# Narrow projections with the activations stationary, an earlier order of first loads, and a reordered ending, in a two-block transformer kernel on one core

## The chip, the cores and the metric

The kernel runs on one core of one Trainium2 chip. The metric is the device time of one execution in microseconds, from its first to its last instruction with what little lies around them. It was timed three times before the change: median 2977.05 us, from 2974.29 to 2977.88.

## The reference

Two blocks run one after the other on 256 tokens of width 2048. The change touches two small projections inside the large input projections, the first loads of the program and its last normalization. Cut to that:

```python
def first_block(x, p, ...):
    a_in = _rmsnorm(h, attn_norm_g[i])
    proj = a_in @ w_in[i]                     # z | xbc | dt_raw (32 columns) | q | k | v
    z, xbc, dt_raw, q, k, v = jnp.split(proj, [o1, o2, o3, o4, o5], axis=-1)
    dt = jax.nn.softplus(dt_raw.astype(jnp.float32) + dt_bias[i].astype(jnp.float32))
    ...                                       # SSM, attention, gated FFN, PLE

def second_block(x, g_mix, w_in, ...):
    h = rms_norm(x, g_mix[l])
    proj = h @ w_in[l]
    q, k, v, z, f, scal, gates = jnp.split(proj, SPLIT_POINTS, axis=-1)   # scal: 4 * 8 = 32 columns
    ...                                       # gated delta rule, Fourier branch, w_o
    h = rms_norm(x, g_mlp[l])
    x = x + jnp.square(jax.nn.relu(h @ w_mlp_up[l])) @ w_mlp_down[l]
    return rms_norm(x, g_final)
```

## The kernel before

**Tiling.** Tokens lie in TT = 2 tiles of P = 128 partitions, the width in KT = 16 k-tiles, outputs in chunks of NC = 512 columns, DC = 4 chunks to a width of 2048. Every float32 product is done as three fp32r products: the weights are split into w_hi (the cast, on ACT) and w_lo (the rest, on DVE), the activations into a_hi and a_lo, and hi x hi, lo x hi and hi x lo are summed in PSUM.

**The weight stream.** All large weights come in one stream of slabs, each 128 partitions x 1024 floats (512 KB), four slabs to a quad. SP issues a slab's transfer into w_raw when DVE has split the one before it in that place (lo_ready). ACT and DVE both have a `split`, for casts and for rests. PE's `slab` (L2154 to L2166) does the eight matmuls on w_hi (L2159), then the four on w_lo (L2164), with a 128x128 tile of the activations stationary and 512 weight columns moving, and counts slab_done. `chunk` runs eight slabs for one 512-column output, into a pair of PSUM banks (one for each token tile) that pair_free says are empty.

**Narrow projections.** The 32 columns of dt (first block) and the 32 of scal (second block) don't come with the stream. `narrow` on PE projects them between two chunks: the 32 weight columns are stationary, all 256 tokens move, 16 k-tiles x 3 products = 48 matmuls into a 32x256 result. ACT copies that to SBUF (narrow_T, L873; narrow2_T, L1121, semaphore narrow_copied), and PE transposes it to token rows with two transposes (L2241), after which narrow_t lets DVE and ACT read it. PE waits for ACT in the middle of that. In front of the first copy ACT evacuates a chunk and computes the sine and cosine of the rotary angles (L870, L871).

**Opening.** SP issues piece 0 of x (512 columns, 512 KB), slab 0, slab 1, piece 1, slabs 2 and 3, pieces 2 and 3, then eight small tensors. ACT's queue issues the identity, then the rows of the five column gains (gain_rows). POOL first issues load_gain(G_SSM), 1 MB, and then its memsets. PE waits for the identity and gain_rows, transposes the gains and then x (L2187), ACT scales the transposed tiles into a_hi (L784), DVE makes a_lo, ACT casts slab 0, and the first chunk starts.

**Ending.** The last quad is the second half of the last down projection. PE does chunks 0 and 1 of it slab by slab for both token tiles, then tile 0's chunks 2 and 3 and tile 1's chunks 2 and 3 (L2832 to L2834). For each (t, n) DVE adds the sum to h (`add_last_to_h`, L2111), ACT squares it with a row sum (`end_squares`, L1326), DVE multiplies by the final gain (`out_gain`, L2116); when the four squares of a tile are in, DVE makes the mean (L2120, L2121), POOL the root (L750), and ACT or DVE scales (L1330, L2144, L2146). All are in a fixed order on their engines, written out by hand. SP stores tile 0 and two chunks of tile 1, ACT the other two chunks as one transfer (L1349).

Of the kernel before, what the change touches and what calls it, by code (L numbers as in the profile page):

```python
# [25 lines left out]
ALU = mybir.AluOpType  # L26
AX = mybir.AxisListType


P = 128  # L30
SEQ, D = 256, 2048
TT = SEQ // P
KT = D // P
NC = 512
# [158 lines left out]
def program(nc, wstream, small, const, out):  # L193

    ctx = ExitStack()
    with ctx:
# [5 lines left out]
        def sem(name):  # L202
            sems[name] = ctx.enter_context(nc.semaphore(name))
            return sems[name]
# [147 lines left out]
        gain_rows = work[:, 0:P]  # L352
        narrow_T = sp[0:HEADS, 1:5].rearrange("p m n -> p (m n)")
        narrow2_T = s_cv[0:4 * DNH, 0]

# [90 lines left out]
        dve_step, pool_step = sem("dve_step"), sem("pool_step")  # L446
        narrow_mm, narrow_t, narrow_copied = sem("narrow_mm"), sem("narrow_t"), sem("narrow_copied")
        sp_abs, sp_exp, sp_sum, sp_ln = sem("sp_abs"), sem("sp_exp"), sem("sp_sum"), sem("sp_ln")
# [41 lines left out]
        def _(sp_):  # L490
# [5 lines left out]
            def first_slab(s):  # L496
                sp_.dma_start(w_raw[:, s, :], wstream[0, s]).then_inc(raw_loaded[s], 16)
            piece(0)
            first_slab(0)
            first_slab(1)  # L500
# [28 lines left out]


            sp_.wait_ge(out_scaled, DC)
            sp_.dma_start(out[0], xn_m[:, 0]).then_inc(stored, 16)
            for c in range(DC // 2, DC):
                cols = slice(c * NC, (c + 1) * NC)
                sp_.wait_ge(normed, NORMED[G_POST] + 2 * DC + c - DC // 2)
                sp_.dma_start(out[1, :, cols], xn_m[:, 1, cols]).then_inc(stored, 16)
            sp_.wait_ge(stored, (1 + 2 * DC + 2 + DC // 2) * 16)

        @block.gpsimd
        def _(pool):  # L540
            step = Chain(pool, pool_step)

            def load_gain(n):

                if n:
                    pool.wait_ge(normed, NORMED[n - 1])
                pool.dma_start(gain[:], small["gains"][N_COLUMN + n:N_COLUMN + n + 1, :].to_broadcast([P, D])).then_inc(gain_loaded, 16)
# [6 lines left out]
            def norm_root(n):  # L554

                pool.wait_ge(rstd_ready, 2 * n + 1)
                nc.gpsimd.tensor_tensor(rstd[:, n], rstd[:, n], neg_half[:, 0:TT], ALU.pow).then_inc(rstd_ready, 1)  # L557


            load_gain(G_SSM)  # L560
            for p in range(4):
# [5 lines left out]
            for s, n in [(pair_free[p], 2) for p in range(4)] + [(back_evac, 2), (back2_evac, 2), (dn_free, 2), (stored, 16)]:  # L567
                pool.wait_ge(s, n)
            norm_root(N_ATTN)


# [180 lines left out]
        def _(act):  # L752
# [89 lines left out]


            act.dma_start(ident[:], const["ident"]).then_inc(first_loaded, 16)
            act.dma_start(gain_rows, small["gains"].rearrange("n (k p) -> (n k) p", p=P)).then_inc(first_loaded, 16)
            act.wait_ge(gain_t, 1)
# [24 lines left out]
            nc.scalar.activation(cos[:], ang[:, 5], ACT.Sin).then_inc(rope_ready, 1)  # L871
            act.wait_ge(narrow_mm, 1)
            nc.scalar.copy(narrow_T[:], bank[7][0:HEADS, 0:SEQ]).then_inc(narrow_copied, 1)  # L873
            softplus_parts(1, sp)
# [232 lines left out]
            with act.Fori(0, 3) as i:  # L1107
                for k in range(2):
# [10 lines left out]
                    nc.scalar.copy(qkv2[:, 0, bass.ds(c * NC, NC)], bank[6][:]).then_inc(back2_evac, 1)  # L1119
            act.wait_ge(narrow_mm, 2)  # L1120
            nc.scalar.copy(narrow2_T[:], bank[5][0:4 * DNH, 0:SEQ]).then_inc(narrow_copied, 1)  # L1121

            q = Q_F + 2
# [198 lines left out]
            def end_squares(t, n):  # L1322

                act.wait_ge(pair_free[n % 2], 2 * (U_MLP + 2 * j + 2 - n % 2) + 2 * (n // 2) + t + 1)
                cols = slice(n * NC, (n + 1) * NC)
                nc.scalar.activation(xn_m[:, t, cols], h[:, t, cols], ACT.Square, accum_out=stat[:, t, n:n + 1]).then_inc(stat_ready, 1)  # L1326
# [11 lines left out]
            end_squares(0, 3)  # L1338
            act.wait_ge(normed, NORMED[G_POST] + 6)
            act.wait_ge(rstd_ready, 2 * (N_OUT + 1))  # L1340
            for c in range(DC):
                out_chunk(0, c)
            end_squares(1, 2)
            end_squares(1, 3)
            act.wait_ge(rstd_ready, 2 * (N_OUT + 2))
            for c in range(DC // 2):
                out_chunk(1, c)
            act.wait_ge(out_scaled, DC + DC // 2)
            act.dma_start(out[1, :, 0:D // 2], xn_m[:, 1, 0:D // 2]).then_inc(stored, 16)  # L1349

        @block.vector
        def _(dve):
# [764 lines left out]

            def end_mean_square(t):
                dve.wait_ge(stat_ready, TT * DC * N_OUT + 6 + 2 * t)
                step(V.tensor_reduce(mean[:, t:t + 1], stat[:, t], AX.X, ALU.add))  # L2120
                V.tensor_scalar(rstd[:, N_OUT, t:t + 1], mean[:, t:t + 1], 1.0 / D, EPS, ALU.mult, ALU.add).then_inc(rstd_ready, 1)  # L2121
            dve.wait_ge(gain_loaded, 16 * (G_OUT + 1))
            for n in range(2):
                split(N_QUADS - 1, 2 * n, 2 * n + 2)
                dve.wait_ge(slab_done, QUAD * (N_QUADS - 2) + 2 * (n + 1))
                for t in range(TT):
                    add_last_to_h(t, n)
                for t in range(TT):
                    out_gain(t, n)

            for t in range(TT):
                for n in range(2, DC):
                    dve.wait_ge(slab_done, QUAD * (N_QUADS - 1 + t) + 2 * (n - 1))
                    add_last_to_h(t, n)
                    if n == 2:
                        out_gain(t, n)
                end_mean_square(t)
                if t == 0:
                    out_gain(t, DC - 1)
            dve.wait_ge(rstd_ready, 2 * (N_OUT + 2))  # L2140
            for c in range(DC // 2, DC):
                cols = slice(c * NC, (c + 1) * NC)
                if c < DC - 1:
                    last = V.tensor_scalar(xn_m[:, 1, cols], h[:, 1, cols], rstd[:, N_OUT, 1:2], None, ALU.mult)  # L2144
                else:
                    last = V.scalar_tensor_tensor(xn_m[:, 1, cols], h[:, 1, cols], rstd[:, N_OUT, 1:2], gain[:, cols], ALU.mult, ALU.mult)  # L2146
                last.then_inc(normed, 1)
        @block.tensor
        def _(pe):
# [79 lines left out]

            def narrow(psum, hi, lo, width, done, token_major, transposed):  # L2230


                o = psum[0:width, 0:SEQ]
                for k in range(KT):
                    T.matmul(o, hi[:, k], a_hi[:, k], start=k == 0, stop=False)
                    T.matmul(o, lo[:, k], a_hi[:, k], start=False, stop=False)
                    last = T.matmul(o, hi[:, k], a_lo[:, k], start=False, stop=k == KT - 1)
                last.then_inc(done, 1)
                pe.wait_ge(narrow_copied, transposed)
                for t in range(TT):  # L2240
                    last = T.transpose(psum[:, SEQ + t * width:SEQ + (t + 1) * width], token_major[:, t * P:(t + 1) * P],  # L2241
                                       ident[0:width, 0:width])
                return last
# [28 lines left out]
            pe.wait_ge(narrow_lo_ready, 1)  # L2272
            narrow(bank[7], w32_hi, w32_lo, HEADS, narrow_mm, narrow_T, 1).then_inc(narrow_t, 1)
            with pe.Fori(0, 2) as i:
# [252 lines left out]
            pe.wait_ge(narrow_lo_ready, 2)  # L2527
            narrow(bank[5], s_hi, s_lo, 4 * DNH, narrow_mm, narrow2_T, 2).then_inc(narrow_t, 1)
            chunk(Q_F + 2, 1, U_F, a_hi, a_lo)
# [293 lines left out]
            for t in range(TT):  # L2823
                ts = slice(t * P, (t + 1) * P)
                for n in range(2, DC):
                    pe.wait_ge(pair_free[n % 2], 2 * (use + 3 - n % 2))
                    for i in range(2 * n - QUAD, 2 * n - QUAD + 2):
                        pe.wait_ge(lo_ready, QUAD * (N_QUADS - 1) + i + 1)
                        for k in range(SLAB_KT):
                            tile = 2 * (i % 2) + k  # L2830
                            wh, wl = (x[:, i, k * NC:(k + 1) * NC] for x in (w_hi, w_lo))
                            T.matmul(pair[n % 2][t][:], last_hi[:, tile, ts], wh, start=tile == 0, stop=False)  # L2832
                            T.matmul(pair[n % 2][t][:], last_lo[:, tile, ts], wh, start=False, stop=False)
                            last = T.matmul(pair[n % 2][t][:], last_hi[:, tile, ts], wl, start=False, stop=tile == 3)  # L2834
                        last.then_inc(slab_done, 1)
# [82 lines left out]
```

## Time and profile before

| what | us |
|---|---|
| median of three timed runs | 2977.05 (2974.29 to 2977.88) |
| the profiled execution's own time | 2975.56 |
| its span, first to last instruction | 2973.7 |
| PE busy in the span | 2937.8 |
| DVE busy | 2006.2 |
| ACT busy | 1419.0 |
| POOL busy | 318.5 |

PE is the matmul side of TensorE, PEld its weight loads, which can overlap. Busy time of a pipelined PE overlaps with itself, so that the start of one matmul to the start of the next says more than their durations: a row with x8 covers eight instructions from the start of the first to the end of the last. "Idle before" in brackets names what ended the idle time.

### The profile page before, as it was taken

What the parts mean: (1) busy time and instruction counts of PE and PEld (TensorE: products, weight loads), DVE (VectorE), ACT (ScalarE), POOL (GpSimd) and SP (SyncE); (2) the same over time, 40 slices, a digit from 0 to 9 for tenths busy, and PEclk for the clock granted to TensorE, in tenths of its full rate; (3) what the DMA queues carried; (4) which work ended last, traced back from release to release, by engine and by line L of the source; (5) the groups of instructions that cost most, each with busy time, mean ns of one, the idle gap of its engine ahead of it and who ended that gap; (6) DMA issues with size and microseconds to landing.
All of it is one profiled execution on the core that took longest, in us unless ns stands there. A gap on an engine that the chain in (4) does not pass through costs nothing.

```text
span 2973.7 us, 44205 instructions
## 1 busy us (share of the span) xinstructions
PE 2937.8 (99%) x15407; PEld 2412.2 (81%) x15407; DVE 2006.2 (67%) x2615; ACT 1419.0 (48%) x1838; POOL 318.5 (11%) x274
## 2 busy tenths in 40 slices
PE   8999999999999999999999999999999999999998
PEld 7888777788888888887888877777888888888887
DVE  6765767656677777667678677777655666666666
ACT  6444556644444444445555453344545444444444
POOL 0002970000000000000000064442000000000000
PEclk9999999999999999999999999999999999999999
DMA  6555443456555555554565533333765555555554
GB/s 217 179 188 173 135 168 125 157 194 213 184 188 186 179 194 186 194 190 142 185 226 176 182 114 122 122 123 119 242 218 192 189 191 187 188 190 190 185 191 147
DMA packets 145147, 525.80 MB, mean 177 GB/s; under 512 B 16416, under 2 KB 17184, under 8 KB 144160
## 3 DMA queue, kind: packets, MB, share of 16 engines
q1 hardware_dynamic: 139760, 503.72, 51.2%
q0 software_dynamic: 1536, 11.78, 1.1%
q10 hardware_dynamic: 3760, 9.05, 0.9%
q8 instruction: 62, 1.02, 0.1%
q14 instruction: 29, 0.24, 0.0%
HBM read 516.09 MB, written 8.39 MB: 176 GB/s over the span
## 4 chain that ended last, share of the span: by engine, by line
PE 93%; DVE 2%; POOL 2%; ACT 1%; issue 1%; DMA 0%; DVEq 0%; ACTq 0%; SPq 0%; POOLq 0%
PE bank L2159 56%; PE bank L2164 28%; PE bank L2256 1%; PE bank L2578 1%; PE bank L2187 1%; DVE w_lo L1360 1%; ACT w_hi L759 1%; PE bank L2607 0%; PE bank L2395 0%; POOL xs L602 0%; PE bank L2489 0%; POOL work L627 0%; PE bank L2264 0%; DMA w_raw<-weights 0%; PE bank L2804 0%
## 5 line engine op out<-in xcount | busy, mean ns | idle before, releaser
L1360 DVE TENSOR_TENSOR w_lo<-w_raw,w_hi 128x1024 fp32r<-128x1024 f32 x952 | 1192.2, 1262 | 784.1 <-ACT w_hi L759 783.2
L759 ACT CAST w_hi<-w_raw 128x1024 fp32r<-128x1024 f32 x952 | 1000.2, 1052 | 1400.5 <-PE bank L2164 1376.6
L2159 PE MATMUL bank<-w_hi,a_hi 128*128 128x512 f32 x2784 | 1109.6, 399 | 4.6 <-ACT w_hi L759 2.8
L2159 PE MATMUL bank<-w_hi,a_lo 128*128 128x512 f32 x2784 | 1087.0, 390 | 0.0
L2164 PE MATMUL bank<-w_lo,a_hi 128*128 128x512 f32 x2784 | 750.1, 390 | 0.0
L2159 PEld LDWEIGHTS bank<-w_hi,a_hi 128*128 128x128 f32 x2784 | 523.9, 188 | 121.2 <-issue 10.6
L2164 PEld LDWEIGHTS bank<-w_lo,a_hi 128*128 128x128 f32 x2784 | 523.1, 188 | 110.2
L2159 PEld LDWEIGHTS bank<-w_hi,a_lo 128*128 128x128 f32 x2784 | 524.5, 188 | 104.7 <-issue 1.9
L2159 PE MATMUL bank<-w_hi,m_hi 128*128 128x512 f32 x480 | 186.8, 389 | 0.0
L2159 PE MATMUL bank<-w_hi,m_lo 128*128 128x512 f32 x480 | 186.7, 389 | 0.0
L1432 DVE TENSOR_TENSOR h<-h,bank 128x512 f32<-128x512 f32 x232 | 148.5, 681 | 19.9 <-PE bank L2164 19.9
L2159 PE MATMUL bank<-w_hi,f_hi 128*128 128x512 f32 x352 | 138.8, 394 | 0.0
L2159 PE MATMUL bank<-w_hi,f_lo 128*128 128x512 f32 x352 | 137.1, 389 | 0.0
L557 POOL TENSOR_TENSOR rstd<-rstd,neg_half 128x2 f32<-128x2 f32 x6 | 4.3, 716 | 1214.8 <-DVE rstd L1389 1214.8
L2164 PE MATMUL bank<-w_lo,m_hi 128*128 128x512 f32 x480 | 128.4, 389 | 0.0
L2159 PEld LDWEIGHTS bank<-w_hi,m_hi 128*128 128x128 f32 x480 | 90.1, 188 | 18.7
L2164 PEld LDWEIGHTS bank<-w_lo,m_hi 128*128 128x128 f32 x480 | 90.1, 188 | 18.7
L2159 PEld LDWEIGHTS bank<-w_hi,m_lo 128*128 128x128 f32 x480 | 90.1, 188 | 18.6
L2164 PE MATMUL bank<-w_lo,f_hi 128*128 128x512 f32 x352 | 94.2, 390 | 0.0
L713 POOL TENSOR_TENSOR delta<-delta,level_sb 128x512 f32<-128x512 f32 x40 | 64.8, 1637 | 127.0 <-DVE delta L1947 122.6
L2164 PEld LDWEIGHTS bank<-w_lo,f_hi 128*128 128x128 f32 x352 | 66.1, 188 | 13.9
L2159 PEld LDWEIGHTS bank<-w_hi,f_lo 128*128 128x128 f32 x352 | 66.1, 188 | 13.5 <-issue 0.2
(410 smaller groups left out, 2520.1 us busy)
## 6 DMA issues: line engine op xcount, KB each, us to landing
w_raw<-weights SPq DMA_DIRECT2D x952, 512.0 KB, 4.0
gate<-gate_st ACTq DMA_DIRECT2D x8, 512.0 KB, 3.9
h<-gate ACTq DMA_DIRECT2D x8, 512.0 KB, 5.0
gain<-gains POOLq DMA_DIRECT2D x3, 1024.0 KB, 7.5
h<-x_tok SPq DMA_DIRECT2D x4, 512.0 KB, 10.8
w_proj_sb<-w_proj POOLq DMA_DIRECT2D x1, 2048.0 KB, 9.7
h_rest<-h POOLq DMA_DIRECT2D x1, 2048.0 KB, 8.6
h<-h_rest POOLq DMA_DIRECT2D x1, 2048.0 KB, 9.9
```

The source lines that it names most:

```text
L557: nc.gpsimd.tensor_tensor(rstd[:, n], rstd[:, n], neg_half[:, 0:TT], ALU.pow).then_inc(rstd_ready, 1)
L713: nc.gpsimd.tensor_tensor(hd.mk, hd.m, level[:, k].unsqueeze(1).to_broadcast(shape), ALU.mult).then_inc(dn_mk, 1)
L759: nc.scalar.copy(w_hi[:, s, :], w_raw[:, s, :]).then_inc(hi_ready, 1)
L1360: V.tensor_tensor(w_lo[:, s, :], w_raw[:, s, :], w_hi[:, s, :].bitcast(F32), ALU.subtract).then_inc(lo_ready, 1)
L1432: V.tensor_tensor(h[:, t, col], h[:, t, col], pair[p][t][:], ALU.add).then_inc(pair_free[p], 1)
L2159: T.matmul(psum[t][:], left[:, t * P:(t + 1) * P], wh, start=start and j == 0 and n == 0, stop=False)
L2164: last = T.matmul(psum[t][:], products[j][0][:, t * P:(t + 1) * P], wl, start=False, stop=stop and j == SLAB_KT - 1)
L2187: last = T.transpose(bank[4 + i % 4][:, k * SEQ + t * P:k * SEQ + (t + 1) * P], src[:, t, (2 * i + k) * P:(2 * i + k + 1) * P], ident[:])
L2256: last = T.transpose(bank[first + ct // 2][:, (ct % 2) * SEQ + t * P:(ct % 2) * SEQ + (t + 1) * P], src[:, t, col0 + ct * P:col0 + (ct + 1 ...
L2578: last = T.matmul(out[r, r], left[:, r], right[:, r], start=True, stop=True)
```

## The change

Five things are changed.

- `narrow` makes the activations stationary: for each k-tile and token tile three matmuls with a 128x128 tile of a_hi or a_lo loaded and the 32 weight columns moving, 96 in all, straight into token rows. The 32x256 result, ACT's two copies, the two pairs of transposes and the semaphores for them go.
- On ACT's queue gain_rows goes ahead of the identity, and slab 0 comes third; SP's queue no longer carries slab 0. POOL issues the load of the SSM gain after the first norm's root instead of first.
- On DVE the last adds, gains and splits are reordered: the adds of chunk 1 come ahead of the last two splits, several gains come later, tile 1's mean of the first three chunks is made ahead of its last add, and the last square is folded in by one instruction. DVE takes over tile 0's last output piece, with its gain.
- On ACT the square of (1, 2) comes ahead of tile 0's scalings, of which three remain. The stores of tile 1 become four of 256 KB, three on SP and one on ACT.
- PE's last chunks wait for one token tile's add instead of two, and start a pair of k-tiles' w_hi products before w_lo is ready.

```diff
@@ narrow
-                o = psum[0:width, 0:SEQ]
                 for k in range(KT):
-                    T.matmul(o, hi[:, k], a_hi[:, k], start=k == 0, stop=False)
-                    T.matmul(o, lo[:, k], a_hi[:, k], start=False, stop=False)
-                    last = T.matmul(o, hi[:, k], a_lo[:, k], start=False, stop=k == KT - 1)
-                last.then_inc(done, 1)
-                pe.wait_ge(narrow_copied, transposed)
-                for t in range(TT):
-                    last = T.transpose(psum[:, SEQ + t * width:SEQ + (t + 1) * width], token_major[:, t * P:(t + 1) * P],
-                                       ident[0:width, 0:width])
+                    for t in range(TT):
+                        o, ts = psum[:, SEQ + t * width:SEQ + (t + 1) * width], slice(t * P, (t + 1) * P)
+                        T.matmul(o, a_hi[:, k, ts], hi[:, k], start=k == 0 and t == 0, stop=False)
+                        T.matmul(o, a_lo[:, k, ts], hi[:, k], start=False, stop=False)
+                        last = T.matmul(o, a_hi[:, k, ts], lo[:, k], start=False, stop=k == KT - 1 and t == TT - 1)
@@ ACT, the copies
-            act.wait_ge(narrow_mm, 1)
-            nc.scalar.copy(narrow_T[:], bank[7][0:HEADS, 0:SEQ]).then_inc(narrow_copied, 1)
...
-            act.wait_ge(narrow_mm, 2)
-            nc.scalar.copy(narrow2_T[:], bank[5][0:4 * DNH, 0:SEQ]).then_inc(narrow_copied, 1)
@@ SP, POOL and ACT, opening
             piece(0)
-            first_slab(0)
             first_slab(1)
...
-            load_gain(G_SSM)
...
             norm_root(N_ATTN)
+            load_gain(G_SSM)
...
+            act.dma_start(gain_rows, small["gains"].rearrange("n (k p) -> (n k) p", p=P)).then_inc(first_loaded, 16)
             act.dma_start(ident[:], const["ident"]).then_inc(first_loaded, 16)
-            act.dma_start(gain_rows, small["gains"].rearrange("n (k p) -> (n k) p", p=P)).then_inc(first_loaded, 16)
+            act.dma_start(w_raw[:, 0, :], wstream[0, 0]).then_inc(raw_loaded[0], 16)
@@ SP, ending
+            sp_.wait_ge(out_scaled, DC - 1)
+            sp_.wait_ge(normed, NORMED[G_POST] + 6)
+            sp_.dma_start(out[0], xn_m[:, 0]).then_inc(stored, 16)
...
+            sp_.wait_ge(normed, NORMED[G_POST] + 8)
+            store(2)
             sp_.wait_ge(out_scaled, DC)
+            store(0)
+            sp_.wait_ge(normed, NORMED[G_POST] + 9)
+            store(3)
@@ ACT, ending
             end_squares(0, 3)
-            act.wait_ge(normed, NORMED[G_POST] + 6)
+            end_squares(1, 2)
+            act.wait_ge(normed, NORMED[G_POST] + 5)
             act.wait_ge(rstd_ready, 2 * (N_OUT + 1))
-            for c in range(DC):
+            for c in range(DC - 1):
                 out_chunk(0, c)
-            end_squares(1, 2)
             end_squares(1, 3)
             act.wait_ge(rstd_ready, 2 * (N_OUT + 2))
-            for c in range(DC // 2):
+            for c in range(2):
                 out_chunk(1, c)
-            act.wait_ge(out_scaled, DC + DC // 2)
-            act.dma_start(out[1, :, 0:D // 2], xn_m[:, 1, 0:D // 2]).then_inc(stored, 16)
+            act.wait_ge(out_scaled, DC + 1)
+            act.dma_start(out[1, :, NC:2 * NC], xn_m[:, 1, NC:2 * NC]).then_inc(stored, 16)
@@ DVE, ending (the new order)
+            split(N_QUADS - 1, 0, 2)
             for n in range(2):
                 dve.wait_ge(slab_done, QUAD * (N_QUADS - 2) + 2 * (n + 1))
                 for t in range(TT):
                     add_last_to_h(t, n)
+            split(N_QUADS - 1, 2, 4)
+            dve.wait_ge(gain_loaded, 16 * (G_OUT + 1))
             for t in range(TT):
+                out_gain(t, 0)
+            last_chunk_done(0, 2)
+            for t in range(TT):
+                out_gain(t, 1)
+            last_chunk_done(0, 3)
+            out_gain(0, 2)
+            dve.wait_ge(stat_ready, TT * DC * N_OUT + 6)
+            step(V.tensor_reduce(mean[:, 0:1], stat[:, 0], AX.X, ALU.add))
+            V.tensor_scalar(rstd[:, N_OUT, 0:1], mean[:, 0:1], 1.0 / D, EPS, ALU.mult, ALU.add).then_inc(rstd_ready, 1)
+            last_chunk_done(1, 2)
+            dve.wait_ge(rstd_ready, 2 * (N_OUT + 1))
+            out_piece(0, DC - 1, True)
+            out_gain(1, 2)
+            step(V.tensor_reduce(mean[:, 1:2], stat[:, 1, 0:DC - 1], AX.X, ALU.add))
+            step(V.tensor_scalar(mean[:, 1:2], mean[:, 1:2], 1.0 / D, EPS, ALU.mult, ALU.add))
+            last_chunk_done(1, 3)
+            dve.wait_ge(stat_ready, TT * DC * N_OUT + 8)
+            V.scalar_tensor_tensor(rstd[:, N_OUT, 1:2], stat[:, 1, DC - 1:DC], 1.0 / D, mean[:, 1:2], ALU.mult, ALU.add).then_inc(rstd_ready, 1)
             dve.wait_ge(rstd_ready, 2 * (N_OUT + 2))
+            out_piece(1, 2, False)
+            out_piece(1, 3, True)
@@ PE, last chunks
-                    pe.wait_ge(pair_free[n % 2], 2 * (use + 3 - n % 2))
+                    pe.wait_ge(pair_free[n % 2], 2 * (use + 3 - n % 2) - 1 + t)
```

## Rows read from the trace of the kernel before

**Rows 1.** The page: busy time and share by engine, and the chain that ended last
```profile
PE 2937.8 (99%) x15407; PEld 2412.2 (81%) x15407; DVE 2006.2 (67%) x2615; ACT 1419.0 (48%) x1838; POOL 318.5 (11%) x274
...
PE 93%; DVE 2%; POOL 2%; ACT 1%; issue 1%; DMA 0%; DVEq 0%; ACTq 0%; SPq 0%; POOLq 0%
```

**Rows 2.** Timeline around the first narrow projection: start us, us, engine line op
```profile
38.02 0.28 PE L2235 MATMUL bank<-a_hi,w_hi 128*32 128x256 f32 x1
...
46.59 0.80 PE L2159 MATMUL bank<-w_hi,a_hi 128*128 128x512 f32 x1
...
49.72 0.39 PE L2159 MATMUL bank<-w_hi,a_lo 128*128 128x512 f32 x1
```

**Rows 3.** Stretches: start:end, length, busy by engine, granted clock, DMA share, GB/s
```profile
43.79:46.25 2.46, 0.00 (x1) 0.01 (x1) 2.46 (x3) 2.41 (x6) 0.00 (x0) 1.00 0.64 201
46.59:49.60 3.01, 3.01 (x8) 2.43 (x8) 2.55 (x9) 2.20 (x3) 0.00 (x0) 0.50 0.91 302
...
1709.84:1712.43 2.59, 2.59 (x25) 2.59 (x24) 2.59 (x1) 2.32 (x2) 2.10 (x1) 1.00 0.02 6
```

**Rows 4.** Timeline around the second narrow projection
```profile
1657.94 1.07 PE L2164 MATMUL bank<-w_lo,a_hi 128*128 128x512 f32 x4
...
1659.64 0.36 PE L2235 MATMUL bank<-a_hi,s_hi 128*32 128x256 f32 x1
...
1665.94 0.20 PEld L2241 LDWEIGHTS bank<-ident_sb,s_cv 32*128 32x128 f32 x2 [0.73 <-ACT s_cv L1121]
...
1666.18 0.50 PE L2159 MATMUL bank<-w_hi,a_hi 128*128 128x512 f32 x1
```

**Rows 5.** Small products and weight loads: timelines, and groups (busy us, mean ns)
```profile
1710.20 0.37 PE L2537 MATMUL bank<-g,cum_sb 128*128 128x8 f32 x2
...
1711.98 0.60 PE L2541 MATMUL bank<-g,chunk_ones_sb 128*128 128x16 f32 x4
...
L2235 PEld LDWEIGHTS bank<-a_hi,w_hi 128*32 128x32 f32 x16 | 1.7, 108 | 0.2
...
L2164 PEld LDWEIGHTS bank<-w_lo,a_hi 128*128 128x128 f32 x2784 | 523.1, 188 | 110.2
...
2900.55 1.12 PE L2804 MATMUL bank<-a_hi,w_lo 128*128 128x256 f32 x8
```

**Rows 6.** Opening: timeline, piece 0's landing, POOL's queue from 6 to 7, a stretch
```profile
0.73 0.67 SPq L494 DMA_DIRECT2D h<-x_tok  x1
...
6.33 0.47 PE L2270 MATMUL bank<-ident_sb,work 128*128 128x128 f32 x1 [6.33 <-DMA work<-gains]
...
10.09 1.04 ACT L759 CAST w_hi<-w_raw 128x1024 fp32r<-128x1024 f32 x1 [1.50 <-DMA w_raw<-weights]
...
11.28 0.77 PE L2159 MATMUL bank<-w_hi,a_hi 128*128 128x512 f32 x1 [2.77 <-ACT w_hi L759]
...
DMA to landing us min/median/max: 5.4/5.4/5.4
...
q0 software_dynamic: 35, 0.29, 68.2%
...
6.00:11.00 5.00, 2.18 (x9) 1.78 (x9) 0.88 (x2) 1.97 (x4) 0.00 (x0) 1.00 1.01 415
```

**Rows 7.** Timeline of the end
```profile
2951.62 2.40 DVE L1360 TENSOR_TENSOR w_lo<-w_raw,w_hi 128x1024 fp32r<-128x1024 f32 x2 [0.24 <-ACT w_hi L759]
...
2953.94 1.40 DVE L2111 SCALAR_TENSOR_TENSOR h<-bank,ms_m,h 128x512 f32<-128x512 f32 x2
...
2955.40 0.50 PE L2832 MATMUL bank<-w_hi,last_hi 128*128 128x512 f32 x1 [1.06 <-DVE h L2111]
...
2965.10 0.69 DVE L2116 TENSOR_TENSOR h<-h,gain 128x512 f32<-128x512 f32 x1 [3.07 <-ACT xn_m L1326]
...
2968.25 1.34 ACT L1330 ACTIVATE xn_m<-h,rstd 128x512 f32<-128x512 f32 x2 [1.04 <-POOL rstd L750]
...
2969.62 0.37 ACTq L1349 DMA_DIRECT2D out<-xn_m  x1
```

## What the change was expected to do

> **What bounds the kernel now.** I read the page first: PE is busy for 99% of the span, DVE 67%, ACT 48%, and 93% of the chain that ended last is PE [rows 1]. So a microsecond taken from PE's own stream in the middle of the program is a microsecond of the span, one added is one lost, and DVE, ACT and the DMA queues count only where PE stands still. The three places that the change touches are then read in the timelines, because there PE does stand still: the opening (first weight matmul at 11.28 us), the narrow projection at 38 us, and the last 20 us. The second narrow projection, at 1660 us, has almost no idle time.
>
> **Narrow projections, now.** The first one starts at 38.02; its 48 products, each 256 moving columns over 32 stationary ones, take until 43.79 (0.12 us each). PE then idles 2.46 us, because ACT is still at other work when they end and copies the 32x256 result late; two transposes follow at 46.25, and the next chunk starts at 46.59: 8.57 us in all [rows 2, 3]. The idle time costs more than itself. The granted clock is 1.00 up to 46, and 0.50, its lower level of 1.2 GHz, from 46.59 to 49.60 [rows 3]. The first eight matmuls of the chunk take 3.13 us for seven spacings (46.59 to 49.72) [rows 2]; at full clock a spacing is (1.07-0.39)/3 = 0.227 us [rows 4] and seven take 1.6. That is 1.5 us more. The second projection runs from 1659.64 to 1666.18, 6.54 us, at full clock, with a wait of 0.73 us ahead of its transposes' loads [rows 4].
>
> **Narrow projections, changed.** 16 k-tiles x 2 token tiles x 3 products make 96 matmuls with 32 moving columns and 128 stationary ones, in the order a_hi, a_lo, a_hi, so no load can be shared. What does one cost when nearly all of it is the load? No product here has 32 moving columns of fp32r. The nearest rows are the 24 small products at 1709.84: 128x128 stationary, 8 or 16 columns moving. Sixteen of them lie between 1710.20 and 1711.98: 1.78/16 = 0.111 us each [rows 5]. That is a load's time, not streaming. It holds for fp32r: a load of 32 columns lasts 108 ns, of 128 columns 188 ns, so 96 columns more take 80 ns, 0.83 ns a column, 0.107 us for 128 [rows 5]. Upper end 0.120 us (fp32r products with 256 moving columns over 128 stationary ones: (1.12-0.28)/7) [rows 5]; lower end 0.065 (the two 32-row transposes' loads, x2 in 0.20 us, the last some 0.136 long) [rows 4]. I take 0.111: 96 x 0.111 = 10.7 us. The trade is therefore a bad one: a quarter of the columns stream, but the loads, which hid behind 256 columns, are four times as wide and twice as many.
> First projection: 10.7 - 8.57 = +2.1; the idle gap and with it the slow start go, -1.5: **+0.6**. Second: 10.7 - 6.54 = **+4.2**. Both if the clock stays at its full level. The ACT copies that go save nothing more, ACT is not the bound.
> The Trainium skill, "TensorE: Matmul & The Clock Gate", section "LDWEIGHTS (loading the stationary operand)", gives a load as its columns divided by 1.2 per ns, whatever the rows; it would give 107 ns, and the trace's spacing of 0.111 agrees. The Trainium skill, same title, section "Weight-path perf modes — Fast Weight Load (FWL) and DoubleRow", says that a fast load switches in by itself for 128 columns when the type isn't FP32, which speaks for this change if fp32r counts as another type; the 188 ns, in line with the 108 for 32 columns, speak against it.
>
> **Opening.** PE waits for the norm weights and the identity together, so their order alone gains nothing: PE's first transpose starts at 6.33 with the norm weights, and piece 0 of x, issued at 0.73, landed 5.4 us later, at 6.1 [rows 6]. Then ACT scales, is free at 8.6 and waits 1.50 for slab 0, cast at 10.09; PE starts at 11.28 [rows 6]. Slab 0 now is the third transfer on ACT's queue instead of the second on SP's, and the 1 MB gain load that shared the engines goes (68% of the engines' time from 6 to 7 us) [rows 6]. Without it 0.5 MB follow on the norm weights at half of some 415 GB/s [rows 6], 2.5 us: about 8.7. So the cast starts near 8.7: **-1.4**. It can't gain more than 1.49 unless the first transposes move, and those are held by piece 0 as well; it gains nothing if slab 0 still lands at 10. Bounds 0 and -2. The pieces behind it on SP each move up one place. The gain load goes to POOL's queue behind the root at 40.5, where POOL next waits for the SSM part; its first reader is in the SSM part too, so it costs 0; in the weight stream there is room for it, 201 GB/s in the stretch from 43.79 against the 415 reached here [rows 3, 6].
>
> **End.** Now the two adds of chunk 1 sit behind two slab splits on DVE; PE waits 1.06 us for them and resumes at 2955.40. Later the square of (1,2) sits behind four scalings on ACT; DVE's multiplication waits 3.07 us for it and only then, after 2965.7, comes the last add. The last scalings start at 2968.25, ACT's last store of 512 KB at 2969.62, 4.1 before the span's end. With the new order, by durations of these rows (add 0.70, gain 0.69, split 1.20, scaling 0.67; a square, by estimate a scaling and the reading of its sum, 0.8) [rows 7]: adds of chunk 1 at 2951.2 to 2952.6; slabs split by 2955.0; PE never waits and ends 1.2 earlier, about 2962.5. DVE then is the bound: gains, adds (0,2), (0,3) to 2959.2, mean to 2960.4, add (1,2), the piece (0,3), gain (1,2), mean to 2963.3, last add until 2964.0. Square until 2964.8, sum 2965.0, root 0.65: scalings at 2965.7 in place of 2968.25, 2.5 less. ACT's last store is half the size: 256 KB less at 415 GB/s are 0.6, and with four stores at once I take 0.4. **-2.9**, between -1.2 (PE's stall only, if the 1 MB store of tile 0 still blocks the queue) and -3.6.
>
> **Sum at full clock:** -1.4 + 0.6 + 4.2 - 2.9 = +0.5, so 2976.1 from the profiled 2975.56. The median of the three timed runs is 2977.05, 1.5 above that execution, and the runs spread 3.6.
>
> **Does the clock stay up?** Here lies most of the uncertainty. At 43.79 to 46.25 PE did nothing and the clock had fallen at the end of it [rows 3]. In the new projections PE is never idle, but it streams 32 columns in each 0.111 us, where its usual rate is 256 in 0.117: an eighth of the array's work, for 10.7 us. The nearest thing to it now is the stretch from 1709.84 to 1712.43: it streams still less, lasts 2.59 us, longer than the idle time that took the clock down, and stays at 1.00 [rows 3, 5]. That speaks for occupancy as what counts, and I follow it; but it is a quarter of the new length, and full work stands on both sides of it. If what counts is work, the clock falls inside each projection. The Trainium skill, same title, part "PE-mode transpose", says that transposes don't count as busy in the way that other matmuls do, which would speak for work over occupancy; no row here shows it.
> Price: at the lower clock a spacing doubles (3.13/7 = 0.447 against 0.227 [rows 2, 4]), and I take a load to do the same. Estimate of the fall: between 2.5 us (the idle time that sufficed) and 5.8 (as long as an old projection), 4.1 us in. The other 6.6 take 13.2, +6.6, and the next chunk pays 1.5 as at 46.59: +8.1 each, +16.2 for both. Ends: 2 x 6.4 = 12.8 and 2 x 9.7 = 19.4.
>
> **Rivals.**
> A, my forecast: loads bound the projections and the clock stays: 2976.1, rounded to **2976**; own range 2972.5 to 2982 (upper end: 0.120 a matmul adds 1.7, a weak opening 1.4, a weak end 1.7; lower end: the better bounds of opening and end, and the opening's slow stretch, which can fall otherwise in another run). For it: the 2.59 us at 1709.84, and PE occupied without a gap. Chance 0.48.
> B, slower: loads bound and the clock falls in both. 2975.56 + 0.5 + 16.2 = 2992.3; 2986 to 2998; 2984 if it falls in one only. It decides from the moment at which a stream of loads counts as rest. For it: by work done, the new projections are nearer to idling than to anything that ran so long at full clock. Against it: 1709.84. Chance 0.36.
> C, faster: 128-column fp32r loads are cheaper when little streams. At 0.065: 6.2 us each, -3.9 and -0.3, sum -8.5: 2967. It is faster by over 0.2% below 0.078 us a matmul, where the projections (192 x 0.078 - 16.7 = -1.7) and the -4.3 of opening and end make -6.0. Against it stand 0.111 and 188 ns. Chance 0.14, for no row has fp32r loads with so little behind them.
> D: a part doesn't do what it says (the opening still waits for slab 0, the end for tile 0's store): +3.1, inside A. The last 0.02 lie above 2998.
>
> **How the numbers follow.** The likeliest is A, 2976; one rival of each sign stands beside it. The range takes A, nearly all of B and the weak side of C: 2970 to 2996. About 0.2% is what a measurement of this kernel can tell from no change, 5.95 us: C lies under 2971.1, B over 2983, A within, with 0.02 of it on either side. Faster 0.15, same 0.46, slower 0.39.
>
> **What would show it.** Spacing of the narrow matmuls: 0.111 (A, B at full clock) or near 0.065 (C). Granted clock inside the two projections and just after: 1.00 (A), 0.50 for some 16 us in each (B). The first projection's wait for ACT's copy gone. PE's first weight matmul near 9.9. No PE idle time at 2955, last scalings 2.5 us closer to PE's last slab than now. I am wrong by 16 us if the clock falls, and by 9 if a 128-column load is cheaper than all rows say.

## The result, and the profile after

The changed kernel took 2991.09 us (median of 5 runs, 2990.90 to 2992.77), against 2977.05 before (5 runs by now, 2974.29 to 2977.88). The ratio is 1.0048, 95% interval 1.0037 to 1.0060: slower, by 14 us. The profiled execution has a span of 2989.3 us where before it was 2973.7, so 15.6 us are to be found. The page of the changed kernel, busy time and the chain that ended last:

```profile
PE 2961.0 (99%) x15499; PEld 2436.6 (82%) x15499; DVE 2004.0 (67%) x2616; ACT 1418.0 (47%) x1835; POOL 317.2 (11%) x274
...
PE 94%; POOL 2%; DVE 2%; issue 1%; ACT 1%; DMA 0%; ACTq 0%; DVEq 0%; POOLq 0%
```

Against [rows 1], DVE, ACT and POOL are as busy as they were. PE is busy for 23 us more, with 92 more matmuls. The loss lies in PE's stream.

The first narrow projection in the timeline (start us, us, engine line op):

```profile
37.55 0.18 PE L2246 MATMUL bank<-w_hi,a_hi 128*128 128x32 f32 x1
...
42.38 0.26 PE L2248 MATMUL bank<-w_lo,a_hi 128*128 128x32 f32 x1
...
42.83 0.37 PE L2248 MATMUL bank<-w_lo,a_hi 128*128 128x32 f32 x1
...
43.05 0.37 PE L2246 MATMUL bank<-w_hi,a_hi 128*128 128x32 f32 x1
...
53.28 0.77 PE L2170 MATMUL bank<-w_hi,a_hi 128*128 128x512 f32 x1
```

The same in two stretches (start:end, length, busy of PE, PEld, DVE, ACT, POOL, granted clock, DMA share, GB/s):

```profile
37.55:42.49 4.94, 4.94 (x46) 4.93 (x45) 2.64 (x14) 4.94 (x11) 1.38 (x2) 1.00 0.30 80
42.49:53.28 10.79, 10.79 (x53) 10.79 (x53) 4.71 (x5) 4.23 (x6) 0.00 (x0) 0.50 0.70 281
```

Until 42.49 the products start 0.11 us apart, after it 0.21: the granted clock goes from 1.00 to 0.50, the level of 1.2 GHz, while PE is busy without a gap. 4.94 us at the full clock and 10.79 at half make 15.7 us where [rows 2] have 8.57. The second projection does the same (1666.28 to 1682.70, 16.4 us, the clock falling near 1670.7) and leaves the next chunk in the low clock too:

```profile
1666.28 0.26 PE L2246 MATMUL bank<-s_hi,a_hi 128*128 128x32 f32 x1
...
1670.30 0.26 PE L2246 MATMUL bank<-s_hi,a_hi 128*128 128x32 f32 x1
...
1671.18 0.37 PE L2246 MATMUL bank<-s_hi,a_hi 128*128 128x32 f32 x1
...
1682.70 0.77 PE L2170 MATMUL bank<-w_hi,a_hi 128*128 128x512 f32 x1
...
1683.28 0.63 PE L2170 MATMUL bank<-w_hi,a_lo 128*128 128x512 f32 x1
```

The opening and the ending, to be held against [rows 6] and [rows 7] and, for the last quad, against this row of the kernel before:

```profile
2951.46 0.39 PE L2832 MATMUL bank<-w_hi,last_hi 128*128 128x512 f32 x1
```

In the changed kernel:

```profile
6.58 0.47 PE L2276 MATMUL bank<-ident_sb,work 128*128 128x128 f32 x1 [6.58 <-DMA ident_sb<-c_ident]
...
9.43 1.04 ACT L763 CAST w_hi<-w_raw 128x1024 fp32r<-128x1024 f32 x1 [0.57 <-DMA w_raw<-weights]
...
10.62 0.77 PE L2170 MATMUL bank<-w_hi,a_hi 128*128 128x512 f32 x1 [1.85 <-ACT w_hi L763]
...
2969.49 0.39 PE L2838 MATMUL bank<-w_hi,last_hi 128*128 128x512 f32 x1
...
2981.52 0.35 SPq L530 DMA_DIRECT2D out<-xn_m  x1
...
2983.04 1.33 ACT L1330 ACTIVATE xn_m<-h,rstd 128x512 f32<-128x512 f32 x2 [0.86 <-POOL rstd L754]
...
2984.40 0.39 ACTq L1349 DMA_DIRECT2D out<-xn_m  x1
```

The wait for slab 0 shrank from 1.50 to 0.57 us, and PE never waits in its last chunks. Cut at the same instructions, the two spans compare so (the last quad's tile-wise part begins at 2951.46 before and 2969.49 after):

| stretch | before | after | difference | forecast |
|---|---|---|---|---|
| start to the first narrow product | 38.02 | 37.55 | -0.47 | -1.4 |
| first projection, to the next chunk | 8.57 | 15.73 | +7.16 | +2.1 |
| from there to the second projection | 1613.05 | 1613.00 | -0.05 | -1.5 |
| second projection | 6.54 | 16.42 | +9.88 | +4.2 |
| from there to the last quad | 1285.28 | 1286.79 | +1.51 | 0 |
| last quad to the end | 22.24 | 19.81 | -2.43 | -2.9 |
| sum | 2973.7 | 2989.3 | +15.6 | +0.5 |

The +1.51 is a balance. The next chunk's first twelve products, in the low clock, take 5.2 us (1682.70 to 1687.91) instead of 2.7; the clock falls once more at 1732.2, for 3.4 us, which is 1.5 us of work; and PE doesn't wait any more where it waited for DVE before (1.25 us at 1724.85, 0.68 us at 2004.24).

### The profile page after: what moved, and what is told of

It reads as the page before. It is cut to its first block, busy times and chain, and to the rows that moved or that the text cites. A ratio compares the mean times of both kernels' runs of the same rounds, so it can differ in the third digit from the quotient of the medians.

```text
span 2989.3 us, 44390 instructions
## 1 busy us (share of the span) xinstructions
PE 2961.0 (99%) x15499; PEld 2436.6 (82%) x15499; DVE 2004.0 (67%) x2616; ACT 1418.0 (47%) x1835; POOL 317.2 (11%) x274
## 4 chain that ended last, share of the span: by engine, by line
PE 94%; POOL 2%; DVE 2%; issue 1%; ACT 1%; DMA 0%; ACTq 0%; DVEq 0%; POOLq 0%
PE bank L2170 56%; PE bank L2175 28%; PE bank L2262 1%; PE bank L2584 1%; PE bank L2198 1%; DVE w_lo L1360 1%; PE bank L2613 0%; ACT w_hi L763 0%; PE bank L2401 0%; POOL xs L606 0%; PE bank L2247 0%; PE bank L2248 0%; PE bank L2495 0%; PE bank L2246 0%; POOL work L631 0%
```

## The experiments

Every kernel was timed beside the kernel before on its chip; ratios are to that.

**The projections, taken out and put in alone.** The first kernel is the changed one with the old `narrow` and its two copies; the second is the kernel before with the new `narrow` only.

> The changed kernel with the old narrow projections (32 columns stationary, 256 tokens moving, ACT's copy, two transposes); opening and ending stay as changed. If the narrow projections carry the whole loss, it is faster than the kernel before by what the profile of the changed kernel shows for its opening (first weight matmul 0.7 us earlier) and its ending (about 2.5 to 2.9 us): 2973.5, between 2972 and 2975. If the opening or the ending has a hidden price, it is at 2977 or above.

> The kernel before with the new narrow projections alone. If they carry the loss: 2977 + 17 = 2994, 3 above the changed kernel; in the profile two stretches of 96 products, at 0.111 us each for some 5 us, then 0.213. If the clock falls only because of something in the new opening: 2982 at most.

Without them: 2973.27 us against 2976.43, ratio 0.9991 (0.9982 to 1.0001); the medians lie 3.2 apart, the profiled spans 2.8, and the interval still holds 1, so this gain is not clear of noise. Alone: 2994.95, ratio 1.0068 (1.0051 to 1.0085). The whole loss is theirs, and it is 18 us; opening and ending give some 3 to 4 back.

**Work or occupancy.** Why does the clock fall while PE is never idle? The next kernel keeps the 96 loads and only streams more behind each: the 32 weight columns four times over.

```diff
-                        o, ts = psum[:, SEQ + t * width:SEQ + (t + 1) * width], slice(t * P, (t + 1) * P)
-                        T.matmul(o, a_hi[:, k, ts], hi[:, k], start=k == 0 and t == 0, stop=False)
+                        o, ts = psum[:, SEQ + (4 * t - 3) * width:SEQ + (4 * t + 1) * width], slice(t * P, (t + 1) * P)
+                        h4, l4 = (x[:, k].unsqueeze(1).to_broadcast([P, 4, width]) for x in (hi, lo))
+                        o = o.rearrange("p (r w) -> p r w", r=4)
+                        T.matmul(o, a_hi[:, k, ts], h4, start=k == 0 and t == 0, stop=False)
...
```

> The changed kernel, in which each narrow product moves its 32 weight columns four times over (128 moving columns, into 128 PSUM columns of which 32 are read; three quarters of the products are not needed). The same 96 loads of 128 columns. Theory W (the clock falls because the array does little work, however occupied PE is): spacing stays at 0.111 to 0.12, since the load is the longer part, but the clock stays at 1.00 and the time falls by some 14 us to 2977, although four times the columns stream. Rival L (a stream of nothing but loads at this density takes the clock down, whatever streams): 0.111, then 0.213, and 2991 as before. Rival S (streaming sets the spacing, not the load): spacing above 0.15 and a time above 2995.

2977.90 us, ratio 1.0005 (0.9996 to 1.0015): 13 us faster than the changed kernel for doing four times the arithmetic in the projections. Its timeline:

```profile
39.61 0.28 PE L2248 MATMUL bank<-w_hi,a_hi 128*128 128x128 f32 x1
39.72 0.28 PE L2249 MATMUL bank<-w_hi,a_lo 128*128 128x128 f32 x1
```

And its first projection as one stretch, cut 0.2 us late at both ends (columns as above):

```profile
37.50:48.20 10.70, 10.70 (x97) 10.70 (x97) 7.36 (x19) 8.98 (x15) 1.38 (x2) 1.00 0.63 230
```

The spacing is 0.11 with 128 columns as with 32, so the load sets it and rival S is out. PE and PEld are busy in both kernels from end to end; the clock stays at 1.00 in this one alone. So it is not occupancy that holds it. Whether it is the number of moving columns or the work in the array is not told apart: the four copies raise both.

This kernel is also the forecast's case A made real: loads bound, clock up. The first product of each projection and of the chunk behind it:

```profile
37.32 0.22 PE L2248 MATMUL bank<-w_hi,a_hi 128*128 128x128 f32 x1
...
47.99 0.44 PE L2170 MATMUL bank<-w_hi,a_hi 128*128 128x512 f32 x1
...
1659.63 0.31 PE L2248 MATMUL bank<-s_hi,a_hi 128*128 128x128 f32 x1
...
1670.38 0.45 PE L2170 MATMUL bank<-w_hi,a_hi 128*128 128x512 f32 x1
```

The projections take 10.67 and 10.75 us, +2.1 and +4.2 as forecast; the stretch between them takes 1611.6 us, 1.4 less than in the kernel before, which is the slow start that was to go. With an opening of -0.7 and an ending of -2.4 the span is 2974.5, where the forecast had 2973.7 + 0.5.

**Spread between full work.** The second projection's products ahead of the next chunk's slabs, 24 to each of four slabs, then 12 to each of eight:

```diff
...
-            narrow(bank[5], s_hi, s_lo, 4 * DNH).then_inc(narrow_t, 1)
-            chunk(Q_F + 2, 1, U_F, a_hi, a_lo)
+            chunk(Q_F + 2, 1, U_F, a_hi, a_lo,
+                  between={n: lambda n=n: narrow(bank[5], s_hi, s_lo, 4 * DNH, 4 * n, 4 * n + 4) for n in range(4)})
```

> The changed kernel, with the second narrow projection's 96 products spread over the first four slabs of the next chunk, 24 ahead of each. The same products and loads. Theory W: the full slabs between keep the clock at 1.00 there, so the second projection costs 96 x 0.111 = 10.7 us instead of about 16 and the slow start behind it goes: some 7 us less, 2984. The first projection, untouched, still pays. Rival: the clock falls from the number of small products, wherever they lie: 2991.

2989.91, ratio 1.0047 (1.0031 to 1.0064): 1.2 under the changed kernel by the medians, 3.2 by the profiled spans (2986.1), not 7. The timeline from the second group on shows where the rest went:

```profile
1673.33 0.26 PE L2248 MATMUL bank<-s_lo,a_hi 128*128 128x32 f32 x1
...
1675.79 0.49 PE L2170 MATMUL bank<-w_hi,a_hi 128*128 128x512 f32 x1
1676.12 0.40 PE L2170 MATMUL bank<-w_hi,a_lo 128*128 128x512 f32 x1
...
1677.08 0.63 PE L2170 MATMUL bank<-w_hi,a_lo 128*128 128x512 f32 x1
...
1678.36 1.91 PE L2175 MATMUL bank<-w_lo,a_hi 128*128 128x512 f32 x4
...
1680.59 0.26 PE L2247 MATMUL bank<-s_hi,a_lo 128*128 128x32 f32 x1
...
1683.85 0.63 PE L2170 MATMUL bank<-w_hi,a_hi 128*128 128x512 f32 x1
...
1691.02 0.63 PE L2170 MATMUL bank<-w_hi,a_hi 128*128 128x512 f32 x1
```

The small products run at 0.11 (but the first few of the group at 1680), yet the clock falls behind them, in the middle of a full slab (0.63 us for 0.40, 1.91 for 1.07), and comes back 3.4 us later. It does so behind the second, the third and the fourth group (three times, and not twice, as the next expectation has it), some 1.6 us lost each time, and not behind the first. Full products that last as long as the small ones between them, 2.7 us each, don't protect.

> As the kernel with the second projection spread over four slabs, but over all eight, 12 small products (1.3 us) ahead of each slab's 2.7 us of full ones. There, with 24 at a time, the clock still fell twice. Theory W: with twice the work for each small product it stays at 1.00, and PE needs 7 us less than in the changed kernel; but ACT and DVE now get the result only at the chunk's end, and their next casts stand behind it: a stall of 3 to 5 us in the next chunk. 2985 to 2989. If the clock falls even so: 2990 or more.

2990.47, ratio 1.0048 (1.0033 to 1.0064), above the range expected. The clock part came true and the price was put too low. Two stretches inside the spread and one behind it (columns as above):

```profile
1672.00:1676.00 4.00, 4.00 (x25) 3.49 (x24) 1.23 (x1) 0.94 (x2) 0.00 (x0) 1.00 0.38 146
...
1688.00:1692.00 4.00, 4.00 (x25) 3.49 (x25) 0.00 (x0) 0.00 (x0) 0.00 (x0) 1.00 0.19 78
...
1704.00:1708.00 4.00, 4.00 (x10) 3.13 (x11) 4.00 (x4) 4.00 (x5) 0.00 (x0) 0.50 0.45 146
```

The product that resumes after it, in the timeline, with the idle time before it and what released it:

```profile
1703.78 0.77 PE L2170 MATMUL bank<-w_hi,a_hi 128*128 128x512 f32 x1 [3.86 <-ACT w_hi L763]
```

And DVE's wait for the result, in the view of waits (engine, waiting group, releaser: us in all, count, longest):

```profile
DVE sp L1840 <- PE bank L2248: 11.2, 1, 11.2
```

With 1.3 us of small products to 2.7 of full ones the clock stays at 1.00 through the whole spread, 30 us. But DVE waits 11.2 us for the result with its next splits queued behind that wait, and ACT behind DVE; PE then idles 3.9 us, and the clock falls after all. I had priced the stall and not the slow start that it brings.

**The opening.** Two kernels, each the one with the old projections and one step of the opening undone.

> The kernel with the old projections and the new opening and ending, but POOL's 1 MB gain load issued first again. It tells how much of the opening's gain comes from that load's move. By the forecast's reasoning slab 0 shares the engines with it again: cast at 10.5 to 11 instead of 9.5, first weight matmul 1 us later. If the load never mattered: no later than 10.8.

> The same, with POOL's load late but slab 0 second on SP's queue as before the change. If the place on ACT's queue is what helps: slab 0 lands at 10, cast at 10.1. If it was the gain load alone: cast at 9.5 or sooner, since on SP slab 0 has only piece 0 ahead of it.

The chain of waits up to 14 us, its long DMA piece (start us, us, what). With the gain load early:

```profile
1.66 10.37 DMA w_raw<-weights
```

With it late and slab 0 on ACT's queue (the kernel with the old projections):

```profile
1.66 7.88 DMA w_raw<-weights
```

With slab 0 on SP the chain goes by the tokens instead:

```profile
0.73 6.70 DMA h<-x_tok
```

and slab 0's cast stands in its timeline so:

```profile
9.43 1.04 ACT L766 CAST w_hi<-w_raw 128x1024 fp32r<-128x1024 f32 x1
```

With the gain load early, slab 0 lands at 12.0 (10.5 to 11 expected), two microseconds later than in the kernel before: third on ACT's queue it suffers more from that load than second on SP's. With the load late the place hardly matters: on SP the cast starts at 9.43, without a wait for slab 0 but behind ACT's scaling, which the tokens' landing (7.4) holds up, against 9.56 on ACT; PE's first weight matmul comes at 10.63 and 10.75. The move of slab 0 gains nothing; the move of the gain load is the gain. These are one run each (2974.94 and 2973.49), told by their traces and not by their times.

**A cheaper old form.** The rows say that 32 stationary columns under 256 moving ones leave room. High and low part side by side as 64 stationary columns let a_hi move once for both:

```diff
...
+                both, one = psum[0:2 * width, 0:SEQ], psum[0:width, 0:SEQ]
                 for k in range(KT):
-                    T.matmul(o, hi[:, k], a_hi[:, k], start=k == 0, stop=False)
-                    T.matmul(o, lo[:, k], a_hi[:, k], start=False, stop=False)
-                    last = T.matmul(o, hi[:, k], a_lo[:, k], start=False, stop=k == KT - 1)
+                    if k == 0:
+                        T.matmul(both, hl[:, k], a_hi[:, k], start=True, stop=False)
+                    T.matmul(one, hl[:, k, 0:width], a_lo[:, k], start=False, stop=False)
+                    if k:
+                        last = T.matmul(both, hl[:, k], a_hi[:, k], start=False, stop=k == KT - 1)
...
```

> The old form of the projections made cheaper, with the new opening and ending: the high and the low part of the 32 weight columns lie side by side as 64 stationary columns, so a_hi moves once for both (32 products of 256 columns instead of 48), the two halves are added by the transposes, and ACT copies the first result right after its casts, ahead of the chunk's evacuation and the sine and cosine. By the rows: 16 x 0.117 = 1.9 us less in each projection, 2.0 less idle time at the first (0.4 left, as at the second), and with so short a pause no slow start, 1.5: from 2973.3 down by 7.3 to 2966. If the clock falls although the pause is short: 2967.5. If 64 stationary columns cost as much as the 16 products save: 2969.7.

2970.02, ratio 0.9978 (0.9969 to 0.9987): faster than both kernels, but 4 us short of what was expected. The 64 columns cost nothing (0.12 us a product). Two other terms failed; the timeline, and the stretch behind the pause:

```profile
42.45 0.37 ACT L873 COPY sp<-bank 64x256 f32<-64x256 f32 x1
...
42.87 1.07 PE L2261 MATMUL bank<-ident_sb,sp 64*128 64x32 f32 x8 [2.09 <-ACT sp L873]
```
```profile
42.50:46.00 3.50, 3.13 (x14) 2.67 (x15) 3.50 (x4) 3.45 (x7) 0.00 (x0) 0.77 0.91 327
```

The projection ended earlier, ACT's four casts did not, so the pause is still 2.09 us (2.46 before the change) and the clock fell as before. And the four adding transposes take 1.0 us, where the two of the old form take 0.34 (46.25 to 46.59): as plain f32 products each runs as two matmuls with a load of its own (x8). The last kernel puts the copy between the second and third cast:

```diff
-            split(q + 2)
+            split(q + 2, 0, 2)
             act.wait_ge(narrow_mm, 1)
             nc.scalar.copy(narrow_T[:], bank[7][0:2 * HEADS, 0:SEQ]).then_inc(narrow_copied, 1)
+            split(q + 2, 2, 4)
```

> The kernel with the fused projections, but ACT's copy of the first result stands between the second and the third of its four casts. In that kernel the projection ended near 40.8 and the copy came only at 42.45, behind four casts; PE idled 2.09 us and the clock fell to 0.5 at 44.4. Now the second cast ends near 40.6, the copy near 41.3: 0.5 us of idle time, as at the second projection, which keeps its clock. 1.6 + 1.5 = 3.1 less: 2970.0 becomes 2966.9. If the casts behind it come too late for PE's next chunk: 2968 to 2970. If the clock falls for another reason than the pause: 2968.4.

2969.16, ratio 0.9974 (0.9964 to 0.9985), not the 2966.9 expected; against the kernel without this edit the difference, 0.9 us, can't be told from none. The pause and the clock behind it did what was expected, and half of the gain went elsewhere; timeline and stretch again:

```profile
42.04 1.07 PE L2262 MATMUL bank<-ident_sb,sp 64*128 64x32 f32 x8 [0.46 <-ACT sp L873]
...
67.56 1.06 PE L2286 MATMUL bank<-ident_sb,cv_act 128*128 128x128 f32 x8 [1.55 <-ACT cv_act L893]
```
```profile
42.00:45.50 3.50, 3.46 (x19) 3.00 (x20) 3.50 (x5) 3.48 (x4) 0.00 (x0) 1.00 0.85 335
```

The pause is 0.46 us and the clock stays up. The 1.6 us of the pause are won: projection to next chunk takes 5.39 us (37.66 to 43.05) against 7.03 (36.85 to 43.88). But the 1.5 us of the slow start come back one chunk later as a wait of 1.55 us for the SiLU on ACT, which the kernel without the edit doesn't have. The SiLU starts 28.6 us behind the projection's first product in both kernels (65.47 - 36.85, 66.26 - 37.66); PE has come 3 us closer to it.

The profiled spans, 2967.1 us with the edit and 2966.3 without, hide the 1.6 us that it won. Behind 1706 us this one is 1.3 us longer: 0.9 of that is a wait of PE for DVE near 2000, and 0.3 is left of a fall of the clock at 1708.3 (1.5 us of work, less a wait of 1.24 us for DVE that it makes needless). And its opening is 0.8 us longer, because the clock came up later in the first chunk. The eighth product of that chunk, without the edit and with it:

```profile
13.79 0.39 PE L2177 MATMUL bank<-w_hi,a_lo 128*128 128x512 f32 x1
```
```profile
13.91 0.63 PE L2178 MATMUL bank<-w_hi,a_lo 128*128 128x512 f32 x1
...
14.34 1.54 PE L2183 MATMUL bank<-w_lo,a_hi 128*128 128x512 f32 x4
```

## Why the prediction was wrong

**The forecast's step that failed** is "Does the clock stay up?". I took the stretch at 1709.84 as speaking for occupancy because it is longer (2.59 us) than the idle time that had sufficed for a fall (2.46), and followed it. It does not bear that, for two reasons.

The kernel with four copies shows that an occupied PE loses its clock or keeps it by what it streams: with 32 moving columns the undivided first projection lost it in each of the four profiles that have it, 4.6 to 5.8 us in, and with 128 columns it kept it for all 10.7.

And 1709.84 was one draw. The same 24 small products, 2.59 us between full slabs, run in every kernel. In six of the eleven profiles the clock stays up behind them; in five (the changed kernel, the new projections alone, the four copies, slab 0 on SP, the copy between casts) it falls in their last half microsecond or within 1 us of their end. The kernel with the old projections and the one with slab 0 on SP have the same program here. The products and what follows them, first in the former:

```profile
1709.52:1712.12 2.60, 2.60 (x26) 2.59 (x24) 2.60 (x1) 2.33 (x2) 2.12 (x1) 1.00 0.01 5
1712.12:1715.50 3.38, 3.38 (x17) 2.79 (x17) 3.38 (x3) 1.55 (x4) 0.00 (x0) 1.00 0.47 149
```
```profile
1709.89:1712.48 2.59, 2.59 (x25) 2.59 (x24) 2.59 (x1) 2.32 (x2) 2.12 (x1) 1.00 0.00 0
1712.50:1715.90 3.40, 3.40 (x10) 2.72 (x10) 3.40 (x3) 1.27 (x2) 0.00 (x0) 0.50 0.47 148
```

The spread kernels say the same: groups of 1.3 us between full work kept the clock, groups of 2.7 us did once and three times not. What decides between the two outcomes for one and the same program stays open. I had written as a reservation that the stretch is a quarter of the new length with full work at both sides.

Rival B, which I gave 0.36, is what happened. That its time is so close (2992.3 forecast, 2991.1 measured) is in part luck. It had 8.1 us of penalty for each projection; measured are 6.5 in the first (15.73 - 10.7 = 5.0, and the 1.5 of a slow start that stayed) and 7.2 in the second (16.42 - 10.7 = 5.7, and the 1.5 of the stretch behind it), 2.5 less in all. Opening and ending in turn gave 1.4 less than forecast, and the two errors nearly cancel.

**What held.** The load as the price of a product: 0.111 us forecast, 0.11 measured in the changed kernel and the same under four times the columns. The Trainium skill, "TensorE: Matmul & The Clock Gate", section "LDWEIGHTS (loading the stationary operand)", has columns divided by 1.2 per ns, which for 128 makes 107 ns, and the trace's 0.11 us agrees. Rival C is out with it: the Trainium skill, same title, section "Weight-path perf modes — Fast Weight Load (FWL) and DoubleRow", has a fast load for full-width weights that aren't FP32, and at 0.11 us no fp32r load here was fast. At the lower clock the spacing nearly doubled, to 0.21. The fall came 4.9 and 4.5 us into the projections, within my 2.5 to 5.8.

**The first projection's slow start, -1.5**, didn't appear in A's favour, since the clock was low at its end here as well. The size was right: the kernel with four copies has its 1.4 (1611.6 us between the projections for 1613.05), and PE doesn't wait for the SiLU there. The last kernel shows where such a gain ends: with PE 3 us ahead at that place, 1.5 us come back as a wait for the SiLU.

**Opening, -1.4.** Measured -0.47 until the first narrow product. Slab 0 was cast and PE's first weight matmul started 0.66 earlier, since slab 0 landed at 9.4 and not at 8.7, where half of 415 GB/s from 6.2 on had put it. From 6 to 9.4 the engines moved 411 GB/s, as much as I had them at, 1.4 MB in all, and slab 0's 0.5 MB are little more than a third of that. Another 0.2 went in the first chunk, which starts in the low clock in both kernels: its products stay 0.43 us apart until 15.5 before and 15.3 after, so that an earlier start had more of them at that price. (A stretch's granted clock reads 1.00 there, as in [rows 6], because the clock's record begins only with the rise; the spacing tells.) The reason given was half wrong: the queue that slab 0 is on brings nothing, the absence of the gain load does.

**Ending, -2.9.** Measured -2.43. The last scalings start 13.55 us after the last quad's tile-wise part begins (2983.04 - 2969.49) and not 16.79 (2968.25 - 2951.46), 3.2 less where I had 2.5. But they are followed by 6.3 us instead of 5.4: tile 0's 1 MB store is issued only at 2981.52 and tile 1's four come behind it within 3 us. ACT's last store, 256 KB, takes 3.8 us to land, where the 512 KB of the kernel before took 3.7. The last term, -0.4 for a smaller last store, had the wrong sign: the part behind the scalings' start is 0.8 longer.

## What to carry to other kernels

Price a TensorE product by the longer of its stationary load and its moving columns, and put the wide operand on the moving side: 96 loads of 128 columns for 32 moving ones cost 10.7 us at full clock where 48 narrow loads under 256 columns cost 5.8. A run of products that are nearly all load can lose the clock, however full PE's row in the profile is; look for the granted clock inside such a run, not only after pauses. One trace in which it stayed up is one draw: look for the same stretch in other traces before you build on it. And a slow stretch that you remove may have been the cover of another engine's chain: look for the wait one chunk later before you book the gain.

## What the runs showed of the hardware that I had not expected

- Streaming more can be faster: 128 moving columns instead of 32 behind each load took 13 us off the kernel (2991.1 to 2977.9), since the clock stayed at 1.00.
- The clock can fall behind a group of small products, in full work that follows: at 1677 in the kernel that spreads them over four slabs, and behind one and the same group of 24 in five profiles of eleven.
- A plain f32 product runs as two matmuls, each with its load at 0.11 us (four products as x8 in 1.07 us). The 24 small ones at 1709.84 in [rows 5] were 12 products in this sense; the price per matmul was unhurt by it.
- The same opening can end 0.8 us apart: with the first weight matmul at 10.76 and 10.79, the two fused kernels reached their first narrow product at 36.85 and 37.66. The clock came up at 13.7 in the one and at 15.3 in the other; 1.6 us more at half the clock are 0.8 us of work.
